# A two-layer decoder trunk on one core: norm sums with tokens on the partitions, inverse root applied behind the up projection, residual sums on two engines, down projection split throughout

## What is computed

```
def rms_norm(x, w):
    y = xf * lax.rsqrt(jnp.mean(xf * xf, axis=-1, keepdims=True) + EPS)
    return y * w
def layer(x, pos, w, st):
    mix, new_state = token_mix(rms_norm(x, w['norm_mix_pre']), pos, w, st)
    x = x + rms_norm(mix, w['norm_mix_post'])
    u = rms_norm(x, w['norm_ffn_pre']) @ w['ffn_up']
    u, ffn_buf = causal_dwconv(u, buf, w['ffn_conv_w'], w['ffn_conv_b'])
    val, gte = jnp.split(u, 2, axis=-1)
    f = (val * jax.nn.gelu(gte, approximate=True)) @ w['ffn_down']
    x = x + rms_norm(f, w['norm_ffn_post'])
```

## Time and profile before

| | us |
|---|---|
| median of 3 runs | 2695.93 (2694.45 to 2698.84) |
| the profiled execution, its own time | 2697.95 |
| its span | 2696.2 |
| TensorE busy in it | 2325.0 (86%) |
| VectorE busy | 1275.7 (47%) |
| ACT busy | 1019.1 (38%) |
| GpSimd busy | 309.4 (11%) |
| end of the output projection, first layer | 899.0 |
| up projection in full flow from | 939.0 |
| down projection's end, first layer | 1333.8 |
| input projection of the second layer in full flow from | 1372.9 |
| end of the last matmul of the down projection, second layer | 2668.3 |

### The profile page before, as it was taken

How to read it: one execution, slowest core, us unless ns; L and a number is a source line. 1 busy time by engine, 2 the same in 40 slices (tenths; PEclk the granted TensorE clock), 3 DMA queues, 4 the chain that set the end, 5 groups by cost and what they waited for, 6 DMA issues and landing times.

```text
span 2696.2 us, 40311 instructions
## 1 busy us (share of the span) xinstructions
PE 2325.0 (86%) x15834; PEld 2004.2 (74%) x15834; DVE 1275.7 (47%) x2039; ACT 1019.1 (38%) x1538; POOL 309.4 (11%) x322
## 2 busy tenths in 40 slices
PE   6979868888989699999888797689798896999996
PEld 5739746566768699989785496556676686999895
DVE  3387842232225666662345877413213346666523
ACT  3213334335433355552232233244344334555521
POOL 0003312232200000000000142123221000000000
PEclk9989978898989899999999798888889998999998
DMA  4362361122234122222314524511222431222221
GB/s 152 99 214 86 124 197 54 48 81 66 66 103 149 47 87 95 95 88 80 107 55 137 171 92 144 170 48 59 75 70 59 136 125 41 95 88 94 87 87 55
DMA packets 113696, 264.59 MB, mean 98 GB/s; under 512 B 14739, under 2 KB 49075, under 8 KB 112611
## 3 DMA queue, kind: packets, MB, share of 16 engines
q1 hardware_dynamic: 107138, 252.96, 29.6%
q10 hardware_dynamic: 6368, 9.05, 1.0%
HBM read 234.21 MB, written 27.76 MB: 97 GB/s over the span
## 4 chain that ended last, share of the span: by engine, by line
PE 62%; DVE 14%; ACT 7%; SPq 5%; issue 4%; DMA 4%; POOL 3%; ACTq 0%; DVEq 0%; POOLq 0%
PE PS L522 37%; PE PS L609 8%; PE PS L994 3%; SPq L414 3%; DVE TM L1588 2%; DVE M L1587 2%; PE PS L949 2%; DVE S L1404 2%; SPq L473 2%; PE PS L852 2%; POOL WL L1824 1%; ACT WH L1037 1%; DVE F L1401 1%; POOL F L1818 1%; PE PS L905 1%
## 5 line engine op out<-in xcount | busy, mean ns | idle before, releaser
L522 PE MATMUL PS<-XH,WH 128*128 128x260 f32 x2592 | 537.5, 289 | 50.6 <-DVE XL L1401 35.2
L522 PE MATMUL PS<-XL,WH 128*128 128x260 f32 x2592 | 527.8, 285 | 5.5 <-issue 5.5
L522 PE MATMUL PS<-XH,WL 128*128 128x260 f32 x2592 | 526.0, 284 | 0.0
L1037 ACT ACTIVATE WH<-R 128x1024 fp32r<-128x1024 f32 x270 | 286.0, 1059 | 622.1 <-PE PS L522 549.8
L522 PEld LDWEIGHTS PS<-XH,WH 128*128 128x128 f32 x2592 | 406.3, 191 | 59.2 <-issue 47.7
L1425 DVE TENSOR_TENSOR WL<-R,WH 128x1024 fp32r<-128x1024 f32 x172 | 210.9, 1226 | 422.1 <-ACT WH L1037 421.4
L522 PEld LDWEIGHTS PS<-XL,WH 128*128 128x128 f32 x2592 | 405.3, 191 | 5.9 <-issue 5.9
L522 PEld LDWEIGHTS PS<-XH,WL 128*128 128x128 f32 x2592 | 403.8, 191 | 0.0
L609 PE MATMUL PS<-XH,WH 128*128 128x260 f32 x1024 | 314.7, 307 | 22.0 <-ACT RB L1055 17.8
L1824 POOL TENSOR_TENSOR WL<-R,WH 128x1024 fp32r<-128x1024 f32 x98 | 232.7, 2374 | 638.5 <-ACT WH L1037 637.6
L609 PE MATMUL PS<-XL,WH 128*128 128x260 f32 x1024 | 301.7, 295 | 0.0
(11 more groups left out here) (318 smaller groups left out, 3043.3 us busy)
## 6 DMA issues: line engine op xcount, KB each, us to landing
R<-w_up SPq DMA_DIRECT2D x88, 512.0 KB, 3.3
R<-k_c SPq DMA_DIRECT2D x128, 256.0 KB, 2.9
R<-w_gate SPq DMA_DIRECT2D x64, 512.0 KB, 3.8
R<-w_proj SPq DMA_DIRECT2D x58, 512.0 KB, 3.3
R<-w_down SPq DMA_DIRECT2D x44, 512.0 KB, 3.3
GATES<-RB SPq DMA_DIRECT2D x128, 130.0 KB, 3.9
S<-GATES SPq DMA_DIRECT2D x64, 260.0 KB, 2.7
S<-v_c SPq DMA_DIRECT2D x64, 192.0 KB, 2.6
```

The source lines that it names most:

```text
L522: i = mm(PS[:, bank + a, 0:HALF], p[:, w, k * 128:(k + 1) * 128], x[:, a * HALF:(a + 1) * HALF], start=first and p is WH and x is hi, stop ...
L1037: do(A(WH[:, half(l, m), :], slot(l, SPLIT[m]), ACT.Copy), w_hi)
```

## The change

Four things change together.

1. **Sums and roots.** The squares of a chunk are now the weights, in pieces of 128 tokens, and the moving operand is one column of ones (`column_sums`): the sums lie with tokens on the partitions, 128x5 (the fifth piece overlaps the fourth and serves the last 8 tokens). Root and reciprocal are taken there (`RS`), and `inverse_root_rows` spreads the result over all partitions again, as rows of 520 columns in PSUM. For j = 1 and 3 the last chunk's squares aren't added by VectorE but summed by TensorE directly; ACT squares that chunk before it copies it; two copies of the rows are made, one for VectorE to read in PSUM, one that ACT copies to `RB`. The post-norm weight goes into ACT's copy out of PSUM. The table for the root is loaded ahead of the output projection (`MX`). The split of the second up tile is made before the root.
2. **Up projection.** It multiplies `X * weight` without the inverse root: ACT makes the leading part from `X`, VectorE the rest in one operation. The first two tiles run together (`first_pair`), with the sums of the squares between their blocks; the inverse root is applied by VectorE as it takes each result out of PSUM (`us_ready`), in place of ACT's copy. The input projection keeps its scaled operand and also runs its first two tiles together.
3. **Residual sums.** For j = 1 and 3 GpSimd does chunks 3, 5 and 7 (a product and a sum each), VectorE the other five. The result is stored chunk by chunk. X is loaded in two halves.
4. **Down projection.** All 22 chunks are split, in their natural order. The first ten leading parts have a buffer of their own (`TH`) and are made inside the up loop.

The diff, cut to its core:

```diff
-K_ORDER = [16, 17, 18, 19, 20] + list(range(16)) + [21]
+EARLY = 10
...
+POOL_CHUNKS = [3, 5, 7]
+UP_BANK = [0, 2, 6, 4]
...
+        RS = sb("RS", [128, 5])
...
+        def row(bank):
+
+            return PS[:, bank:bank + 2, :].rearrange("p a c -> p (a c)")[:, 0:TOK]
+
+        def new_x(l, j, k):
+
+            if k in POOL_CHUNKS:
+                return x_pool.nth(l, 3 * (j // 2) + POOL_CHUNKS.index(k))
+            return x_dve.nth(l, 5 * (j // 2) + k - sum(c < k for c in POOL_CHUNKS))
+
+        def hidden_hi(k):
+
+            return TH[:, k, :] if k < EARLY else (XH, XL)[(k - EARLY) // KD][:, (k - EARLY) % KD, :]
...
+            for a in range(2):
+                sp.dma_start(X[:, 4 * a:4 * a + 4, :], x_in[:, 4 * a:4 * a + 4, :]).then_inc(x_loaded[a].sem, 16)
+            sp.dma_start(K[:, :], consts).then_inc(loaded.sem, 16)
...
-            def norm_sum(l, j):
-
-                pe.wait_ge(*sq_added.nth(l, 8 * (j // 2) + 7))
-                for a in range(2):
-                    i = mm(PS[:, 4 + a, 0:HALF], kc(C_ONE), S[:, 2, a * HALF:(a + 1) * HALF], start=True, stop=True)
-                i.then_inc(sum_ready.sem, 1)
-
-            def norm_sum_chunks(l, j):
-
+            def normed(l, j, k):
+
+                pe.wait_ge(*norm_out.nth(l, 4 * j + k))
+
+            def column_sums(chunk, first, last):
+
+                for t in range(5):
+                    lo = min(128 * t, TOK - 128)
+                    ins = mm(PS[:, 4, t:t + 1], chunk[:, lo:lo + 128], one, start=first and t == 0, stop=last and t == 4,
+                             skip_group_check=True)
+                return ins
+
+            def sum_squares(l, j, k):
+
+                pe.wait_ge(*sq_ready.nth(l, 8 * j + k))
+                column_sums(S[:, k % 2, :], k == 0, k == KD - 1).then_inc(sq_summed.sem, 1)
+
+            def sum_added(l, j):
+
+                pe.wait_ge(*sq_added.nth(l, 7 * (j // 2) + 6))
+                column_sums(S[:, 2, :], True, False)
+                pe.wait_ge(*sq_ready.nth(l, 8 * j + 7))
+                column_sums(S[:, 1, :], False, True).then_inc(sum_ready.sem, 1)
+
+            def inverse_root_rows(l, j, *banks):
+
+                pe.wait_ge(*rs_inv.nth(l, j))
+                for bank in banks:
+                    for t in range(5):
+                        n = min(128, TOK - 128 * t)
+                        ins = mm(PS[:, bank + t // 4, 128 * (t % 4):128 * (t % 4) + n],
+                                 RS[:, t:t + 1].to_broadcast([128, 128]), ident[:, 128 - n:128], start=True, stop=True)
+                    finish(ins, rs_row)
+
+            def first_pair(l, tiles, banks, j, beside):
+
+                for n in tiles:
+                    pe.wait_ge(*w_hi.nth(l, split_no[n]))
+                    pe.wait_ge(*lo_ready(l, split_no[n]))
+
+                def step(i, k):
+                    hi, lo = x_parts(k)
+                    ins = block_split(half(l, split_no[tiles[i]]), k, hi, lo, banks[i], k == 0, k == KD - 1)
+                    if k == KD - 1:
+                        ins.then_inc(tile_used.sem, 1)
                 for k in range(KD):
-                    pe.wait_ge(*sq_ready.nth(l, 8 * j + k))
-                    for a in range(2):
-                        i = mm(PS[:, 4 + a, 0:HALF], kc(C_ONE), S[:, k % 2, a * HALF:(a + 1) * HALF],
-                               start=k == 0, stop=k == KD - 1)
-                    i.then_inc(sq_summed.sem, 1)
+                    normed(l, j, k)
+                    step(0, k)
+                    beside(k)
+                    if k >= 3:
+                        step(1, k - 3)
+                for k in range(KD - 3, KD):
+                    step(1, k)
...
-                norm_sum(l, 1)
-                norm_sum_chunks(l, 2)
-
-                for j in range(2 * JF):
-                    if j >= 4:
-                        pe.wait_ge(*up_evac.nth(l, j - 4))
-                    dense_split(l, AT["up", j], 2 * (j % 4), x_parts, *[normed(l, 2)] * (j == 0))
+                sum_added(l, 1)
+                inverse_root_rows(l, 1, 6, 4)
+                first_pair(l, (AT["up", 0], AT["up", 1]), (0, 2), 2, lambda k: sum_squares(l, 2, k))
+                inverse_root_rows(l, 2, 4)
+                for j in range(2, 2 * JF):
+                    if j == 3:
+                        pe.wait_ge(*rs_copied.nth(l, 1))
+                    elif j >= 4:
+                        pe.wait_ge(*us_ready.nth(l, j - 4))
+                    dense_split(l, AT["up", j], UP_BANK[j % 4], x_parts)
...
-                        q, bank = K_ORDER[k], 2 * (d % 2)
+                        bank = 2 * (d % 2)
                         if e == 0 or k == 0:
                             pe.wait_ge(*full(l, n))
                             pe.wait_ge(*w_hi.nth(l, m))
                             pe.wait_ge(*lo_ready(l, m))
                         if d == 0:
-                            pe.wait_ge(*h_ready.nth(l, q))
-                        if q < 2 * KD:
-                            if d == 0:
-                                pe.wait_ge(*hd_hi.nth(l, q))
-                                pe.wait_ge(*hd_lo.nth(l, q))
-                            ins = block_split(half(l, m), e, (XH, XL)[q // KD][:, q % KD, :], FR[:, q, :], bank, False,
-                                              False)
-                        else:
-                            for a in range(2):
-                                ins = mm(PS[:, bank + a, 0:HALF], slot(l, n)[:, 128 * e:128 * e + 128],
-                                         F[:, q, a * HALF:(a + 1) * HALF], start=k == 0, stop=k == JF - 1)
+                            pe.wait_ge(*hd_hi.nth(l, k))
+                            pe.wait_ge(*hd_lo.nth(l, k))
+                        ins = block_split(half(l, m), e, hidden_hi(k), FR[:, k, :], bank, k == 0, k == JF - 1)
...
-                do(A(halves(S[:, 3, :]), pair(4), ACT.Sqrt, bias=eps, scale=1.0 / DM), root_ready)
+                do(A(RS[:, :], PS[:, 4, 0:5], ACT.Sqrt, bias=eps, scale=1.0 / DM), root_ready)
...
+                do(A(MX[:, 15:16], eps, ACT.Sqrt))
+
+                def evac(l, j, d, out, weight):
+
+                    def copy():
+                        do(A(halves(F[:, out + d, :]), pair(2 * (d % 2)), ACT.Copy, scale=V[:, l, weight + d:weight + d + 1]))
+                    if d < KD - 1:
+                        copy()
...
+                    if d < KD - 1:
+                        split(l, S_OUT + d + 2)
+                    evac(l, 1, d, 0, V_NPOST)
+                split(l, S_UP + 1)
                 root(l, 1)
-                squares(l, 2, lambda k: act.wait_ge(*norm_out.nth(l, 8 + k)))
+                rows_for_pool(l, 1)
+                for k in range(KD):
+                    act.wait_ge(*new_x(l, 1, k))
+                    do(A(XH[:, k, :], X[:, k, :], ACT.Copy, scale=V[:, l, V_FPRE + k:V_FPRE + k + 1]), xh_ready)
+                    square(l, 2, k)
                 root(l, 2)
-                leading(l, 1)
+                act.wait_ge(*rs_row.nth(l, 3))
+                do(A(RB[:, :], row(4), ACT.Copy), rs_copied)
...
-                        if m >= 2:
-                            act.wait_ge(*fcv.nth(l, m - 2))
-                        else:
-                            act.wait_ge(*norm_out.nth(l, 23))
-                        do(A(halves(S[:, g, :]), pair(2 * (m % 4)), ACT.Copy))
-                        do(A(FO[:, ch, :], S[:, g, NPR - 2:TOK], ACT.Copy))
+                        act.wait_ge(*us_ready.nth(l, m))
                         if j:
                             act.wait_ge(*h_ready.nth(l, j - 1))
-                        do(A(halves(S[:, 2 + g, :]), pair(2 * (m % 4)), ACT.Identity,
+                        do(A(S[:, 2 + g, :], S[:, g, :], ACT.Identity,
                              bias=V[:, l, V_FCB + ch:V_FCB + ch + 1],
                              scale=V[:, l, V_FCW + 3 * ch + 2:V_FCW + 3 * ch + 3]), up_evac)
+                        do(A(FO[:, ch, :], S[:, g, NPR - 2:TOK], ACT.Copy), fo_saved)
+                    if 1 <= j <= EARLY:
+                        do(A(hidden_hi(j - 1), F[:, j - 1, :], ACT.Copy), hd_hi)
                     act.wait_ge(*fcv.nth(l, 2 * j + 1))
...
+            def inverse_root(l, j):
+
                 dve.wait_ge(*root_ready.nth(l, j))
...
-                do(v_.reciprocal(RB[:, :], S[:, 3, :]))
+                do(v_.reciprocal(RS[:, :], RS[:, :]), rs_inv)
...
+            def add_residual(l, j, k, out):
+
+                tt(S[:, 4, :], F[:, out + k, :], row(6), ALU.mult)
+                tt(X[:, k, :], X[:, k, :], S[:, 4, :], ALU.add, x_dve)
...
-                post_norm(l, 1, V_NPOST, 0)
-                pre_norm(l, 2, V_FPRE)
-
+                for k in range(KD - 1):
+                    split(l, S_OUT + k + 2)
+                    add_squares(l, 1, k)
+                split(l, S_UP + 1)
+                inverse_root(l, 1)
+                dve.wait_ge(*rs_row.nth(l, 1))
+
+                def unscaled_rest(k):
```

(34 more changed lines are left out.)

168 lines of the change are left out of this document (86 added, 82 removed).

## The result

| | before | after |
|---|---|---|
| median of 5 runs, us | 2695.93 (2694.45 to 2704.83) | 2677.15 (2672.00 to 2686.63) |
| span of the profiled execution | 2696.2 | 2684.9 |

The ratio is 0.9928 (0.9900 to 0.9956): 19 us faster where 41.4 were forecast, and above the range, which ended at 2668. The profiled execution of after is the slowest of its five, so its span alone gives 11.3 us.

The account below looks back on a forecast made before the run. TensorE was taken to bound the dense stages, a serial chain through three engines the norm stretches and down-projection starts. 2 x (6.2 + 4.1) + 2 x 4.5 + 7.5 + 7.8 - 3.3 = 41.6 us gave 2654.5 us, range 2639 to 2668.

Parts of the forecast that it names:

- Down projection: Seven of eight outputs all split gain 6.2 us per layer; an earlier start of the projection gains 4.1 us per layer.
- the queue of twelve rests: Down projection's start: 12 splits of 0.73 us on VectorE end at +15.5, the third tile's WL at +16.8.
- Up loop: Up projection: VectorE's added scaling and early splits, 9.2 of 11.56 us per pair, stay covered by TensorE; effect 0.
- New sums: Norms: a chunk's sum takes 10 passes of 0.128 us, 1.28 us; bounds 0.7 and, at half clock, 2.56.
- Half clock: Gap from output to up projection: lower TensorE clock costs about 1 us early and 1.5 behind the 3 us wait.
- (c): Rival, 4%: TensorE stays at 1.2 GHz through all sums and first pairs; slower than before, 2730 us.
- Gap: Output to up projection: two tiles finished after 42 us instead of 46.5; gain 4.5 us per layer.
- Boundary: Between the layers: two tiles finished after 37.7 us plus 0.3 for the clock, instead of 45.5; gain 7.5 us.
- The start: Program start: two tiles finished after 52.4 us instead of 49.1; loss 3.3 us.
- Alternation: Residual sums: VectorE's additions and rests wait for whole GpSimd instructions (1.22 us each); without it the gap gains 8.5 us.
- the end: Behind the last matmul: chunk 7 ready at 16.9, stored and landed by 20 us instead of 27.9; gain 7.8 us.
- (b): Rival, 15%: more lost in gaps, sums at half clock at start and boundary, longer waits between VectorE and GpSimd; 2670 us.

Follow-up runs that it names:

- second pair of profiles: Both kernels, before and after, profiled again unaltered; after's ratio to before 0.9918, median 2682.47 beside 2704.99 us.
- down6: Changed kernel with chunks 16 to 21 of every down output again plain FP32 matmuls; ratio to the kernel before 0.9925.
- early3: Changed kernel with the third down tile's split moved between hidden chunks 13 and 15 instead of behind the last; ratio to the kernel before 0.9890.
- Wide sums: Changed kernel whose two pre-norms again sum 260 squares moving past ones, with root and reciprocal of 128x520; ratio to the kernel before 0.9811, again 0.9820.
- cols64: Changed kernel whose sums move 64 columns of ones instead of one; ratio to the kernel before 0.9903.
- one_sum: Changed kernel without the sums of chunks 0 to 6 between first up-tile blocks; up projection ends 280.8 and 281.1 us behind the output projection.
- no_pool: Changed kernel with VectorE doing all eight chunks of both residual sums, GpSimd none; ratio to the kernel before 0.9927.

## Why the prediction was wrong, point by point

- **Down projection: right.** 6.2 + 4.1 = 10.3 us per layer forecast, 10.3 and 9.5 measured, 10.4 and 9.0 in the second pair of profiles; output 15.8 us (15.9), third tile at 17.4 (16.9), wait 4.76 (4.9). The forecast's own rows, 7 x (5.26 - 4.33), give 6.5 and not 6.2, which is also what down6 measures. The forecast took the queue of twelve rests as given; early3 shows that 4 to 5 us more lay in its order.
- **Up loop: right.** In its flow TensorE never waited; 8.8 us of VectorE per pair (9.2).
- **New sums: the step that failed.** It priced a sum at 1.28 us, with 2.56 (the half clock) named as the bound and not taken. At the upper clock 1.17 was measured, so the row chosen was good; but only the sums behind the outputs and the last of each gap had it; all eight at the start and at the boundary and the first four to six of a gap ran at 2.13, and the clock stayed down while they ran. The Trainium skill ("TensorE: Matmul & The Clock Gate", LDWEIGHTS) gives 107 ns a load, 128: 117 a pass was measured at the upper clock, in the middle, and 213 at the lower.
- **Half clock: mis-sized with it.** "About 1 us early and 1.5 behind that wait" was taken from stalls behind which TensorE recovered under blocks. It became 17 us of lower clock in layer 1 and 26 in the profiled layer 2; half clock behind 15 us of a gap was what the prediction had named as the sign of (c). Gap: 4.5 us forecast, 2.0 measured (once -2.5). Boundary: 7.5 forecast, -0.2 measured; the sums began 9.7 us behind the last matmul (8.2), took 17.2 us without a pause (11.3) and ended at 26.9 (19.5), 7.4 late. Chunk 7 was ready at 1355.3 - 1336.8 = 18.5 us (16.9), which cost nothing, since TensorE was still summing earlier chunks. The start: sums to 30.35 (27), row 38.3 (34.7); loss 5.1 and 5.9 (3.3).
- **Alternation: right in kind, small in effect.** Additions 826 ns and rests 1147 on average, and GpSimd's own operations 1.48 and 1.57 us where 1.22 was taken: GpSimd waits too, which the forecast left out. At the end its chunk 7 was ready 18.9 us behind the last matmul (16.9) and the rest took 2.4 us (3.0), which is the 1.2 us missing there (7.8 forecast, 6.6 measured).
- **Rivals.** (b), sums at half clock at start and boundary, was the case, with 15%; its 2670 still lay 7 us low, since it took the blocks and sums of the gaps at the upper clock. (c) had the mechanism for the gaps, but for all of each pair. The fault was one of chances: the forecast let a TensorE that starts at the lower level and is given only one-column passes have the upper one after two sums, while the rows that it had, the old sums of the earlier trace rows and both stalls of the earlier trace rows, show a return under matmuls of 260 columns only.
- **The sum.** In places 20.8 and 24.0 us instead of 41.6. Of the 17.6 missing in the second pair, 7.7 are the boundary, 5.0 the gaps, 2.6 the start, 1.1 the end and 1.2 the down projection. Wide sums alone bring 22.2 us back (1080.7 to 1058.5), more than was missing, and that with their reciprocals paid.

## What to carry to other kernels

Price a new TensorE operation at both clock levels, and ask what TensorE does in the microseconds before it: here the narrow sums filled its time for 17 us and more without the upper level coming back, so the form that spares a reciprocal of 3.40 us in each of these norms cost 22 us more over the program. If an order of an engine's queue removes a wait, look for where it stands next; a backlog of work moves, it does not go. Where long stages scatter by several microseconds from one profile to the next, compare places, not spans.

## What the runs showed of the hardware

- TensorE without a pause in one-column or 64-column passes kept the pass length of its lower level for 17.2 and 17.3 us (start and boundary of after and cols64; granted clock 0.50 at the boundary). Blocks and narrow sums in turn, without a pause, went on at the lower level for 16.6 to 26.7 us (12 gaps); blocks with 260-column sums had the upper one back 3.0 to 6.1 us behind the restart (10 gaps), blocks alone 4.0 and 6.6 us behind the last wait (one_sum). Which difference between the two forms matters isn't settled: they differ in the moving columns, in which operand is the weights and in the share of time spent loading them, and no form between them was run. The Trainium skill ("Perfetto Trace Analysis", Matmul Optimizations) asks that matmuls be issued back to back in batches, since the engine scales its power with its use; by these traces that alone wasn't enough.
- The return of the clock scatters: of the twelve gaps with narrow sums (after twice, cols64, no_pool, early3, down6), three had it back only after 26.5 to 26.7 us and the up projection's end 4 to 5 us later than the others (292.5 against 288 to 289). Why is open.
- GpSimd and VectorE slow each other: in after GpSimd's operation takes 1.28 us alone and 1.62 to 1.64 beside VectorE operations with two SBUF inputs; VectorE's rest takes 1.67 instead of 0.76 and its addition 0.94 instead of 0.70. Products that read PSUM kept 0.70 beside it.
